# Three products by tokens: each tile takes all four units of weights in a row, then the other tile of its pair

## The chip, the cores and the metric

One Trainium2 chip, one of its NeuronCores. The metric is the device time of one execution in microseconds (us). The kernel before ran three times: 3430.88, 3432.21 and 3433.60 us, median 3432.21. One execution was taken by the hardware profiler; it ran 3431.43 us, and its profile covers a span of 3429.9 us.

## The reference, cut to what matters

The program computes two transformer-like blocks one after the other, on a sequence of 512 tokens with a model width of 1024. The first block has two layers of attention and MLP. The second block mixes three branches: a state-space branch (SSD), a delta-rule recurrence (RWKV) and a gated recurrence (HGRN). The change touches three slices of the second block's input product:

```
p = xn @ w_in[l]
z, xbc, dt_raw, p_rwkv, p_hgrn, p_gate = jnp.split(p, in_splits, axis=-1)
...
y = y.reshape(b, L, SSM_INNER) * jax.nn.silu(z)          # state-space branch
...
q, f_fwd, f_bwd, i, g = jnp.split(p, 5, axis=-1)          # gated recurrence; i are its values
```

`z` is 512 x 1024 and is made as two halves of 512 columns; the values `i` ("hgrn v") are 512 x 512. All are needed much later than they are made, so each is written to DRAM and fetched again when its branch ends.

## The kernel before

All matrix products take fp32 operands split in a high and a low part (both rounded to fp32r), and add three matmuls for each 128 rows of the inner dimension: high x high, high x low, low x high.

**Weights.** A class `Stream` brings the weights. They pass through six blocks of SBUF, in turn. Each block takes one load of 512 KB, called a unit here. SyncE issues the load (L381), ScalarE rounds the high part (L361, "split" in this text), VectorE subtracts to get the low part (L368). TensorE waits for the low part. A block is loaded anew only when the unit in it has been used for the last time: SyncE's queue waits on TensorE (mark `used`), and every later entry of that queue waits behind.

**Tokens and Features.** A product with tokens on the partitions is a `Tokens` job, one with features on them a `Features` job. The jobs touched have four units (256 rows of the inner dimension by 512 columns each) and four tiles of 128 tokens. A step is one unit for one tile: two chunks of 128 rows, three matmuls each (L427 to L429), so six matmuls of 512 columns. `together=2` means that the tiles go in two passes, tiles 0 and 1, then 2 and 3, and within a pass unit by unit, both tiles for each unit. A job has 16 steps. The banks of PSUM for these products are two, numbers 0 and 1 (ring "gemm 2"), handed out in turn: tile 2 takes the bank of tile 0, tile 3 that of tile 1, and the next job's first tile that of tile 2.

**Draining.** When a tile's last unit is done, `KeptOut` drains the bank into one of four staging tiles (`probabilities` twice, `gate0`, `gate1`) and SyncE stores it (L2180). For z, ScalarE takes tanh (L2199) and VectorE multiplies (L2208), which frees the bank. For hgrn v ScalarE copies (L2201) and that frees it.

**When units are split.** `Tokens.ahead` says up to which unit ScalarE and VectorE have split when the first tile of a pair takes a unit. In the last pass, at the last unit, it goes one unit further, to the third unit of the next job. That unit's load goes to the block of this job's first unit.

**What sets the order.** A `Plan` gives each step of each stage a time, in steps of products. Each engine's program is the list of all steps sorted by that time. TensorE's part of a scan stage may be put later by some steps (`later`). Beside the z products run pieces of the state-space scan (its decay matmuls L2568 and L2570, its L2601; on ScalarE L2620 and L2630; on VectorE L2668 and L2675), TensorE's share two steps later than the others'. Beside hgrn v run pieces of the RWKV scan, about one between any two steps (L2928, L2905, L2867 on TensorE, L3167 and L3188 on ScalarE, L3027 on VectorE), about one step later. Engines run their lists strictly in order, so a row that waits holds all rows behind it.

## Time and profile before

| what | value |
|---|---|
| median of three runs | 3432.21 us |
| profiled execution | 3431.43 us |
| its span | 3429.9 us |
| TensorE matmul busy | 3310.9 us (97%) |
| VectorE busy | 2018.7 us (59%) |
| ScalarE busy | 1354.2 us (39%) |
| load of a unit, issue to landing, median | 3.8 us |

The span is what the profiler saw, from the first to the last instruction. "Busy" is the time in which an engine had an instruction under way. Matmuls overlap: a matmul of 512 columns is shown with a length of 0.39 us, while one starts each 0.23 us when nothing stops them. The two z products run from 2280.78 us to 2354.5 us of the span, hgrn v from 2639.2 us to 2720.6 us.

### The profile page before, as it was taken

What the parts mean: (1) busy time and instruction counts of PE and PEld (TensorE: products, weight loads), DVE (VectorE), ACT (ScalarE), POOL (GpSimd) and SP (SyncE); (2) the same over time, 40 slices, a digit from 0 to 9 for tenths busy, and PEclk for the clock granted to TensorE, in tenths of its full rate; (3) what the DMA queues carried; (4) which work ended last, traced back from release to release, by engine and by line L of the source; (5) the groups of instructions that cost most, each with busy time, mean ns of one, the idle gap of its engine ahead of it and who ended that gap; (6) DMA issues with size and microseconds to landing.
All of it is one profiled execution on the core that took longest, in us unless ns stands there. A gap on an engine that the chain in (4) does not pass through costs nothing.

```text
span 3429.9 us, 53077 instructions
## 1 busy us (share of the span) xinstructions
PE 3310.9 (97%) x21864; PEld 2720.9 (79%) x21864; DVE 2018.7 (59%) x3803; ACT 1354.2 (39%) x2604; POOL 0.2 (0%) x4
## 2 busy tenths in 40 slices
PE   7989999999999999999999999999999999999998
PEld 7777788888888777788888888777777788888887
DVE  6776753554436776753554438775766678664434
ACT  5456543342225466543343224434443324232222
POOL 0000000000000000000000000000000000000000
PEclk9999999999999999999999999999999999999999
DMA  4221223233324221223233334333411235433332
GB/s 141 80 70 50 56 74 105 92 99 98 98 99 127 86 64 50 57 79 105 86 105 99 96 101 118 89 92 106 125 38 40 92 95 157 135 97 94 97 98 86
DMA packets 353875, 315.31 MB, mean 92 GB/s; under 512 B 10288, under 2 KB 281776, under 8 KB 353636
## 3 DMA queue, kind: packets, MB, share of 16 engines
q1 hardware_dynamic: 352916, 309.75, 29.9%
q8 instruction: 175, 2.87, 0.3%
q10 hardware_dynamic: 720, 2.16, 0.2%
q14 instruction: 64, 0.52, 0.0%
HBM read 288.28 MB, written 23.59 MB: 91 GB/s over the span
## 4 chain that ended last, share of the span: by engine, by line
PE 80%; DVE 11%; ACT 5%; issue 3%; DMA 2%; SPq 0%; DVEq 0%; ACTq 0%
PE banks L532 14%; PE banks L534 13%; PE banks L533 13%; PE banks L427 8%; PE banks L429 8%; PE banks L428 8%; DVE weights_r L368 2%; PE banks L632 1%; ACT weights_high_r L361 1%; PE banks L2928 1%; PE banks L2867 1%; PE banks L1241 1%; PE banks L1228 1%; PE banks L1332 1%; PE banks L2881 1%
## 5 line engine op out<-in xcount | busy, mean ns | idle before, releaser
L368 DVE TENSOR_TENSOR weights_r<-weights,weights_high_r 128x1024 fp32r<-128x1024 f32 (+2 forms) x517 | 592.9, 1154 | 355.7 <-ACT weights_high_r L361 354.6
L532 PE MATMUL banks<-h_T_hi,weights_high_r 128*128 128x512 f32 (+2 forms) x1912 | 759.6, 397 | 10.6 <-DVE h_T_lo L881 4.7
L534 PE MATMUL banks<-h_T_hi,weights_r 128*128 128x512 f32 (+2 forms) x1912 | 737.9, 386 | 0.0
L533 PE MATMUL banks<-h_T_lo,weights_high_r 128*128 128x512 f32 (+2 forms) x1912 | 737.5, 386 | 0.0
L361 ACT ACTIVATE weights_high_r<-weights 128x1024 fp32r<-128x1024 f32 (+2 forms) x517 | 511.2, 1000 | 360.8 <-DMA weights<-in_w_mlp 213.3
L532 PEld LDWEIGHTS banks<-h_T_hi,weights_high_r 128*128 128x128 f32 x1912 | 361.4, 189 | 98.6 <-issue 28.8
L534 PEld LDWEIGHTS banks<-h_T_hi,weights_r 128*128 128x128 f32 x1912 | 361.2, 189 | 72.7
L533 PEld LDWEIGHTS banks<-h_T_lo,weights_high_r 128*128 128x128 f32 x1912 | 361.7, 189 | 68.0 <-issue 2.6
L427 PE MATMUL banks<-weights_high_r,h_T_hi 128*128 128x512 f32 (+2 forms) x672 | 279.3, 416 | 9.2 <-DVE gate L2208 3.7
L429 PE MATMUL banks<-weights_high_r,h_T_lo 128*128 128x512 f32 (+2 forms) x672 | 254.9, 379 | 0.0
L428 PE MATMUL banks<-weights_r,h_T_hi 128*128 128x512 f32 (+2 forms) x672 | 254.7, 379 | 0.0
L602 DVE TENSOR_TENSOR cellsX<-cellsX,banks 128x512 f32<-128x512 f32 x112 | 76.7, 685 | 276.3 <-PE banks L429 276.2
L427 PE MATMUL banks<-weights_high_r,cellsM_r 128*128 128x512 f32 (+1 forms) x464 | 181.6, 391 | 0.0
L428 PE MATMUL banks<-weights_r,cellsM_r 128*128 128x512 f32 (+1 forms) x464 | 178.1, 384 | 0.0
L429 PE MATMUL banks<-weights_high_r,cellsC_r 128*128 128x512 f32 x432 | 169.2, 392 | 0.0
L427 PEld LDWEIGHTS banks<-weights_high_r,h_T_hi 128*128 128x128 f32 x672 | 127.6, 190 | 41.3 <-issue 9.7
L427 PE MATMUL banks<-weights_high_r,cellsE_r 128*128 128x512 f32 x384 | 150.3, 391 | 2.4 <-DVE cellsS L3898 2.4
L428 PE MATMUL banks<-weights_r,cellsE_r 128*128 128x512 f32 x384 | 150.0, 391 | 0.0
L429 PE MATMUL banks<-weights_high_r,cellsB_r 128*128 128x512 f32 x384 | 149.6, 390 | 0.0
L428 PEld LDWEIGHTS banks<-weights_r,h_T_hi 128*128 128x128 f32 x672 | 128.0, 190 | 23.2 <-issue 3.9
L429 PEld LDWEIGHTS banks<-weights_high_r,h_T_lo 128*128 128x128 f32 x672 | 127.5, 190 | 22.9
L1541 DVE TENSOR_TENSOR gate<-gate,banks 128x512 f32<-128x512 f32 x64 | 44.0, 687 | 131.2 <-ACT gate L1533 131.2
(562 smaller groups left out, 5228.5 us busy)
## 6 DMA issues: line engine op xcount, KB each, us to landing
weights<-in_w_in SPq DMA_DIRECT2D x183, 512.0 KB, 3.8
weights<-in_w_mlp SPq DMA_DIRECT2D x128, 512.0 KB, 3.8
weights<-in_ffn_w_in SPq DMA_DIRECT2D x44, 512.0 KB, 3.8
weights<-in_w_out SPq DMA_DIRECT2D x24, 512.0 KB, 3.6
weights<-in_ffn_w_down SPq DMA_DIRECT2D x22, 512.0 KB, 3.5
weights<-in_w_mem_kv SPq DMA_DIRECT2D x16, 512.0 KB, 3.5
weights<-in_w_diff_o SPq DMA_DIRECT2D x16, 512.0 KB, 3.6
weights<-in_w_mla_o SPq DMA_DIRECT2D x8, 512.0 KB, 3.4
```

Of the source, the lines that this page charges most:

```text
L361: ac.e.activation(self.part(c.w_high_r, u), self.part(c.w_raw, u), ACT.Copy).then_inc(*ac.tell("high", u))
L368: ve.e.tensor_tensor(self.part(c.w_raw_r, u), self.part(c.w_raw, u), self.part(c.w_high_r, u).bitcast(F32), ALU.subtract).then_inc(*ve.tel ...
L427: pe.e.matmul(out, lhsT=hi[k][:, tok], rhs=wh[:, j, :], start=(k == 0), stop=False)
L428: pe.e.matmul(out, lhsT=hi[k][:, tok], rhs=wl[:, j, :], start=False, stop=False)
L429: mm = pe.e.matmul(out, lhsT=lo[k][:, tok], rhs=wh[:, j, :], start=False, stop=last)
L532: pe.e.matmul(out, lhsT=wh[:, k, :], rhs=hi[k][:, cols], start=(k == 0), stop=False)
L533: pe.e.matmul(out, lhsT=wh[:, k, :], rhs=lo[k][:, cols], start=False, stop=False)
L534: mm = pe.e.matmul(out, lhsT=wl[:, k, :], rhs=hi[k][:, cols], start=False, stop=(k == self.chunks - 1))
L602: ve.e.tensor_tensor(dst, dst, got, ALU.add).then_inc(*ve.frees(*key))
L632: mm = pe.e.transpose(bank[0:m, at:at + rows], src, c.ident[0:rows, 0:rows])
L1228: mm = pe.e.matmul(bank[:, 0:v[j].shape[-1]], lhsT=c.pT[n % 2][:, j * P:(j + 1) * P], rhs=v[j], start=(j == 0), stop=(j == len(v) - 1))
L1541: ve.e.tensor_tensor(y, y, got, ALU.mult).then_inc(*ve.frees(*key))
```

## The change

`Tokens` gets a parameter `in_a_row`. The units are taken in groups of that many, and within a pass each tile takes a whole group before the other tile of the pair does. With 1, the default, the order is as before. The three jobs (`z 0`, `z 1`, `hgrn v`) are given 4, which is all their units. The other `Tokens` jobs keep 1.

```diff
-    def __init__(..., together=NT, tile_ready=lambda t: ()):
+    def __init__(..., together=NT, tile_ready=lambda t: (), in_a_row=1):
...
+        self.in_a_row = in_a_row
...
         for n, some in enumerate(self.passes):
-            for u in self.units:
+            for some_units in (self.units[j:j + self.in_a_row] for j in range(0, len(self.units), self.in_a_row)):
                 for t in some:
-                    yield n, u, t, t == some[0], u == self.units[-1]
+                    for u in some_units:
+                        yield n, u, t, t == some[0], u == self.units[-1]
...
-            return Tokens(c, name, c.hT, KD, w[:, col:col + 512], sink, ready=normed, ring=ring, together=2)
+            return Tokens(c, name, c.hT, KD, w[:, col:col + 512], sink, ready=normed, ring=ring, together=2, in_a_row=4)
```

Lines of the file behind it move down by one or two: L2199 is L2201 afterwards, L3167 is L3169. Steps of one job, before: u0t0 u0t1 u1t0 u1t1 u2t0 u2t1 u3t0 u3t1, then the same with t2 and t3. Now: u0t0 u1t0 u2t0 u3t0 u0t1 u1t1 u2t1 u3t1, then the same with t2 and t3. On TensorE and SyncE the rows read the same before and after, since a row names neither the unit nor the tile; their waits have other values. On ScalarE and VectorE rows move.

ScalarE, start of the second z product, before. L2199 drains tile 3 of the first z product. `weights4`, `weights5` and `weights0` are the blocks whose loads the splits wait for; L2630 and L2620 belong to the scan.
```order
L2199 ACTIVATE probabilities<-banks 128x512 [waits sp_kept1]
L361 ACTIVATE weights_high_r_50<-weights 128x1024 [waits sp_weights4]
L361 ACTIVATE weights_high_r_50<-weights 128x1024 [waits sp_weights5]
L2630 ACTIVATE cellsE<-banks 128x512 [waits pe_filled]
L2630 ACTIVATE cellsS<-banks 128x512 [waits pe_filled]
L2620 ACTIVATE cellsX_r_51<-small,cellsC 128x128 x4
L2620 ACTIVATE small_r_58<-small,cellsC 128x128 x4
L361 ACTIVATE weights_high_r_50<-weights 128x1024 [waits sp_weights0]
L2199 ACTIVATE gate0<-banks 128x512 [waits sp_kept2,pe_filled]
```
The same place now:
```order
L2201 ACTIVATE probabilities<-banks 128x512 [waits sp_kept1]
L361 ACTIVATE weights_high_r_50<-weights 128x1024 [waits sp_weights4]
L361 ACTIVATE weights_high_r_50<-weights 128x1024 [waits sp_weights5]
L361 ACTIVATE weights_high_r_50<-weights 128x1024 [waits sp_weights0]
L2632 ACTIVATE cellsE<-banks 128x512 [waits pe_filled]
L2632 ACTIVATE cellsS<-banks 128x512 [waits pe_filled]
L2622 ACTIVATE cellsX_r_51<-small,cellsC 128x128 x4
L2622 ACTIVATE small_r_58<-small,cellsC 128x128 x4
L2201 ACTIVATE gate0<-banks 128x512 [waits sp_kept2]
```
The split that waits for `weights0` moved up past the scan's four rows.

VectorE, the same place, before. L2208 frees the bank of tile 3, L368 are the low parts, L2675 and L2668 belong to the scan.
```order
L2208 SCALAR_TENSOR_TENSOR probabilities<-probabilities,banks 128x512 [waits act_tanh]
L368 TENSOR_TENSOR weights_r_49<-weights,weights_high_r_50 128x1024 [waits act_high] x2
L2675 TENSOR_TENSOR cellsE<-cellsE,cellsM 128x512 [waits bank4_freed]
L2668 TENSOR_TENSOR cellsE_r_56<-small,cellsC_r_55 128x512 [waits pe_filled]
L2675 TENSOR_TENSOR cellsS<-cellsS,cellsM 128x512 [waits bank5_freed]
L2668 TENSOR_TENSOR cellsS_r_57<-small,cellsC_r_55 128x512 [waits pe_filled]
L368 TENSOR_TENSOR weights_r_49<-weights,weights_high_r_50 128x1024 [waits act_high]
L2208 SCALAR_TENSOR_TENSOR gate0<-gate0,banks 128x512 [waits act_tanh]
```
Now:
```order
L2210 SCALAR_TENSOR_TENSOR probabilities<-probabilities,banks 128x512 [waits act_tanh]
L368 TENSOR_TENSOR weights_r_49<-weights,weights_high_r_50 128x1024 [waits act_high] x3
L2677 TENSOR_TENSOR cellsE<-cellsE,cellsM 128x512 [waits bank4_freed]
L2670 TENSOR_TENSOR cellsE_r_56<-small,cellsC_r_55 128x512 [waits pe_filled]
L2677 TENSOR_TENSOR cellsS<-cellsS,cellsM 128x512 [waits bank5_freed]
L2670 TENSOR_TENSOR cellsS_r_57<-small,cellsC_r_55 128x512 [waits pe_filled]
L2210 SCALAR_TENSOR_TENSOR gate0<-gate0,banks 128x512 [waits act_tanh]
```
The third low part moved up past the scan's four rows.

ScalarE, second pass of hgrn v, before. L3167 and L3188 belong to the RWKV scan, L2201 drains tile 2, `weights1` is the block of the job's first unit, loaded anew with the third unit of the next job.
```order
L3167 ACTIVATE cellsE<-banks 128x256 [waits pe_filled]
L3167 ACTIVATE cellsS<-banks 128x256 [waits pe_filled]
L3188 ACTIVATE cellsX<-banks 128x256 [waits pe_filled]
L3188 ACTIVATE probabilities<-banks 128x256 [waits pe_filled]
L3167 ACTIVATE cellsE<-banks 128x256 [waits pe_filled]
L3167 ACTIVATE cellsS<-banks 128x256 [waits pe_filled]
L3188 ACTIVATE cellsX<-banks 128x256 [waits pe_filled]
L3188 ACTIVATE probabilities<-banks 128x256 [waits pe_filled]
L3167 ACTIVATE cellsE<-banks 128x256 [waits pe_filled]
L3167 ACTIVATE cellsS<-banks 128x256 [waits pe_filled]
L2201 ACTIVATE probabilities<-banks 128x512 [waits sp_kept0]
L361 ACTIVATE weights_high_r_50<-weights 128x1024 [waits sp_weights1]
```
Now; the first two rows are the two that stand ahead of the first row above:
```order
L3169 ACTIVATE cellsE<-banks 128x256 [waits pe_filled]
L3169 ACTIVATE cellsS<-banks 128x256 [waits pe_filled]
L2203 ACTIVATE probabilities<-banks 128x512 [waits sp_kept0]
L361 ACTIVATE weights_high_r_50<-weights 128x1024 [waits sp_weights1]
L3169 ACTIVATE cellsE<-banks 128x256 [waits pe_filled]
L3169 ACTIVATE cellsS<-banks 128x256 [waits pe_filled]
L3190 ACTIVATE cellsX<-banks 128x256 [waits pe_filled]
L3190 ACTIVATE probabilities<-banks 128x256 [waits pe_filled]
L3169 ACTIVATE cellsE<-banks 128x256 [waits pe_filled]
L3169 ACTIVATE cellsS<-banks 128x256 [waits pe_filled]
```
The drain of tile 2 and the split behind it moved up past ten rows, three rounds of the scan.

VectorE, the same place, before. L3246 and L3027 belong to the scan.
```order
L3246 TENSOR_TENSOR cellsE<-cellsE,banks 128x256 [waits pe_filled]
L3246 TENSOR_TENSOR cellsS<-cellsS,banks 128x256 [waits pe_filled]
L3027 TENSOR_TENSOR cellsX<-banks,small 128x256 [waits pe_filled,act_taken]
L3027 TENSOR_TENSOR cellsX<-banks,small 128x256
L3027 TENSOR_TENSOR cellsX<-banks,small 128x256 [waits pe_filled,act_taken]
L3027 TENSOR_TENSOR probabilities<-banks,small 128x256
```
Now:
```order
L3248 TENSOR_TENSOR cellsE<-cellsE,banks 128x256 [waits pe_filled]
L3248 TENSOR_TENSOR cellsS<-cellsS,banks 128x256 [waits pe_filled]
L368 TENSOR_TENSOR weights_r_49<-weights,weights_high_r_50 128x1024 [waits act_high]
L3029 TENSOR_TENSOR cellsX<-banks,small 128x256 [waits pe_filled,act_taken]
L3029 TENSOR_TENSOR cellsX<-banks,small 128x256
L3029 TENSOR_TENSOR cellsX<-banks,small 128x256 [waits pe_filled,act_taken]
L3029 TENSOR_TENSOR probabilities<-banks,small 128x256
```
The low part of the same unit stands ahead of L3027 (now L3029). Before it stood behind three rounds of the scan as well.

## Rows read from the trace of the kernel before

**Rows 1.** The page: busy time of each engine, and the chain's shares.
```profile
PE 3310.9 (97%) x21864; PEld 2720.9 (79%) x21864; DVE 2018.7 (59%) x3803; ACT 1354.2 (39%) x2604; POOL 0.2 (0%) x4
...
PE 80%; DVE 11%; ACT 5%; issue 3%; DMA 2%; SPq 0%; DVEq 0%; ACTq 0%
```

**Rows 2.** TensorE in time: start us, length us, line, tiles, [idle before <-releaser].
```profile
2285.28 0.39 PE L427 MATMUL banks<-weights_high_r,h_T_hi 128*128 128x512 f32 x1
...
2296.00 0.50 PE L427 MATMUL banks<-weights_high_r,h_T_hi 128*128 128x512 f32 x1 [0.32 <-DVE gate L2208]
...
2300.08 0.50 PE L427 MATMUL banks<-weights_high_r,h_T_hi 128*128 128x512 f32 x1 [1.53 <-DVE gate L2208]
...
2311.09 0.47 PE L427 MATMUL banks<-weights_high_r,h_T_hi 128*128 128x512 f32 x1 [0.22 <-DVE probabilities L2208]
...
2318.94 0.50 PE L427 MATMUL banks<-weights_high_r,h_T_hi 128*128 128x512 f32 x1 [3.39 <-DVE probabilities L2208]
...
2326.62 0.55 PE L2601 MATMUL banks<-cellsE 128*128 128x64 f32 x4
...
2333.97 0.50 PE L427 MATMUL banks<-weights_high_r,h_T_hi 128*128 128x512 f32 x1 [0.82 <-DVE gate L2208]
...
2339.35 0.50 PE L427 MATMUL banks<-weights_high_r,h_T_hi 128*128 128x512 f32 x1 [1.06 <-DVE gate L2208]
...
2354.01 0.39 PE L429 MATMUL banks<-weights_high_r,h_T_lo 128*128 128x512 f32 x1
...
2354.54 0.47 PE L532 MATMUL banks<-h_T_hi,weights_high_r 128*128 128x512 f32 x1
```

**Rows 3.** VectorE in time, same columns, start of both z products.
```profile
2285.20 1.22 DVE L368 TENSOR_TENSOR weights_r<-weights,weights_high_r 128x1024 fp32r<-128x1024 f32 x1
...
2318.20 0.69 DVE L2208 SCALAR_TENSOR_TENSOR probabilities<-probabilities,banks 128x512 f32<-128x512 f32 x1 [3.35 <-ACT probabilities L2199]
2319.14 2.36 DVE L368 TENSOR_TENSOR weights_r<-weights,weights_high_r 128x1024 fp32r<-128x1024 f32 x2 [0.26 <-ACT weights_high_r L361]
2321.42 0.69 DVE L2675 TENSOR_TENSOR cellsE<-cellsE,cellsM 128x512 f32<-128x512 f32 x1
```

**Rows 4.** ScalarE in time, same columns, splits of weights in z.
```profile
2289.65 1.06 ACT L361 ACTIVATE weights_high_r<-weights 128x1024 fp32r<-128x1024 f32 x1 [11.00 <-DMA weights<-in_w_in]
...
2318.07 2.00 ACT L361 ACTIVATE weights_high_r<-weights 128x1024 fp32r<-128x1024 f32 x2
```

**Rows 5.** SyncE's queue in time, loads of weights in z.
```profile
2285.69 0.43 SPq L381 DMA_DIRECT2D weights<-in_w_in  x1
...
2319.30 0.43 SPq L381 DMA_DIRECT2D weights<-in_w_in  x1
```

**Rows 6.** TensorE in time, same columns, in hgrn v.
```profile
2687.40 0.40 PE L429 MATMUL banks<-weights_high_r,h_T_lo 128*128 128x512 f32 x1
...
2706.37 0.40 PE L429 MATMUL banks<-weights_high_r,h_T_lo 128*128 128x512 f32 x1
...
2708.51 0.41 PE L2928 MATMUL banks<-cellsE 64*64 64x64 f32 x16
2709.34 0.46 PE L2928 MATMUL banks<-cellsS 64*64 64x64 f32 x16 [0.41 <-DVE cellsX L3027]
```

**Rows 7.** Busy time by window: length, PE, PEld, DVE, ACT, POOL, PEclk, DMA.
```profile
2639.00:2724.00 85.00, 79.70 (x2219) 65.55 (x2215) 52.51 (x143) 27.56 (x72) 0.00 (x0) 1.00 0.13 37
```

**Rows 8.** SyncE's queue in time, in hgrn v.
```profile
2687.82 0.38 SPq L381 DMA_DIRECT2D weights<-in_w_in  x1
```

**Rows 9.** ScalarE in time, same columns, in hgrn v.
```profile
2707.22 0.39 ACT L3167 ACTIVATE cellsE<-banks 128x256 f32<-128x256 f32 x1 [5.04 <-PE banks L2928]
...
2718.81 1.07 ACT L361 ACTIVATE weights_high_r<-weights 128x1024 fp32r<-128x1024 f32 x1
```

**Rows 10.** VectorE in time, same columns, in hgrn v.
```profile
2708.53 0.76 DVE L3027 TENSOR_TENSOR cellsX<-banks,small 128x256 f32<-128x256 f32 x2 [2.10 <-ACT cellsX L3188]
```

**Rows 11.** Busy time by window, behind the longest wait in z.
```profile
2320.00:2324.00 4.00, 4.00 (x12) 3.17 (x11) 3.91 (x6) 0.06 (x1) 0.00 (x0) 0.57 0.65 175
```

More of the change, by code:

```diff
@@ L386, with __init__ @@
 class Tokens(Stage):
-    def __init__(self, c, tag, xT, chunks, src, sink, ready=(), tiles=NT, ring="gemm", together=NT, tile_ready=lambda t: ()):
+    def __init__(self, c, tag, xT, chunks, src, sink, ready=(), tiles=NT, ring="gemm", together=NT, tile_ready=lambda t: (), in_a_row=1):
         self.c, self.tag, self.xT, self.chunks, self.sink, self.ready, self.tiles = c, tag, xT, chunks, sink, ready, tiles
+        self.in_a_row = in_a_row
         self.ring, self.cols, self.tile_ready = ring, src.shape[1], tile_ready
```

## The prediction

> **What bounds the kernel now.** I read four views. First the page's busy times and the shares of the chain of waits: TensorE is busy 97% of the span and carries 80% of the chain [rows 1]. So an edit pays only where TensorE stands still, or where it makes TensorE stand still. Second, TensorE in order of time over the two z products. Six of their steps start late because the VectorE drain of a PSUM bank (L2208) was late: by 0.32, 1.53, 0.22, 3.39, 0.82 and 1.06 us, 7.34 us in all [rows 2]. The step after them, the first of the next gates, starts with no recorded idle, 0.30 us after the last matmul would have let it (2354.54 against 2354.01 plus 0.23). Third, the drains and weight splits on VectorE and ScalarE and the loads on SyncE around these steps [rows 3 to 5]. Fourth, the same for the product of the recurrence's values, "hgrn v". It has no wait for a bank; each of its steps lies between pieces of the RWKV scan, and TensorE is busy 79.70 of 85.00 us there at full clock, 2.4 GHz [rows 6, 7].
>
> **What the change does not do.** No matmul is added or removed, and the names and sizes of TensorE's and SyncE's instructions stay in place. A Tokens job has 16 steps of six matmuls, numbered 0 to 15 here: the pair (tile 0, tile 1), then the pair (2, 3), each over four units. What moves is when a bank is full, when a unit is first needed, when it is last used, and so where its drain and the splits of later units stand.
>
> **Bank waits removed.** Before, tile 0 is full after step 6 and its bank is wanted at step 8. Now it is full after step 3. Tile 1 is full after step 7 as before, but tile 3 wants its bank at step 12, not 9. A bank then has four steps to be drained instead of one. I remove all but the 0.22: tile 2 of the first z product is now full early, but ScalarE drains it behind the same scan work. Idle is counted from the modelled end of the last matmul; back to back, starts are 0.23 us apart and the modelled length is 0.39, so each wait that goes gives 0.16 more. First z: 0.32 + 1.53 + 2 x 0.16 = 2.2. Second z: its tile-1 start 3.39 + 0.16 = 3.6; then 0.82 + 1.06 + 2 x 0.16 = 2.2; and the 0.30 at its end. Removed in all: 8.3 us.
>
> **New wait 1, low part of the fourth unit, first z.** It was needed at step 6, now at step 3, which TensorE reaches at 2285.28 [rows 2]. VectorE makes it from 2285.20 for 1.22 us, to 2286.42 [rows 3]. Cost 1.2. VectorE is then itself fed by TensorE's next scan matmuls, so the delay is carried on and not made up. First z: 2.2 - 1.2 = 1.0 gained.
>
> **New waits 2 and 3, start of the second z.** Tile 1's late bank no longer stops step 1, but step 3 now wants the low part of unit 3. VectorE makes it right behind the late drain: from 2319.14, one of two halves of 2.36, so ready about 2320.4 [rows 3]. TensorE would have gone on at 2318.94 - 3.58 = 2315.4, and two steps of 1.37 take it to 2318.1: it waits 2.3 there. Then the splits of the units after next: in the order above the one that waits for weights0 has moved up on both engines, ahead of the scan's L2675. Its load is issued at 2319.30, behind the store of tile 3 [rows 5]. A load issued at 2285.69 let its waiting split start at 2289.65, 3.96 us later [rows 4, 5], so this one starts at 2323.26, takes 1.06, VectorE's half about 1.15, and L2675 starts at 2325.5 instead of 2321.42 and ends 0.69 later, at 2326.2. TensorE's L2601, which reads it, stood at 2326.62 [rows 2]. Of the 3.6 removed 0.4 is left. All this is relative to the scan matmuls before it, so the 1.0 of the first product stays on top. Sum of z: 1.0 + 0.4 + 2.2 + 0.3 = 3.9 us gained. Bounds: all 8.3 if neither queue was late; 0.5 if the price of a lowered clock (below) is added twice.
>
> **New wait 4, hgrn v.** This is the cost. Unit 0's block of weights is now used last in step 12 (tile 3), not step 9. The split of unit 6, whose load needs that block, moved the other way: from behind step 14 to behind step 11. On ScalarE it stood at 2718.81, behind three more rounds of the scan [rows 9]. Now it stands before the L3167 that ran at 2707.22 (L3169 in the changed file). Behind it in that queue are L3167 and L3188, on which TensorE's L2928 and VectorE's L3027 wait; VectorE's half stands before L3027 too. Step 12 ends at 2706.37 + 0.40 = 2706.77 [rows 6]. In the kernel before the load that waited for step 9 (last matmul 2687.40 + 0.40) was issued at 2687.82 [rows 6, 8]. So: issue 2706.8, landed and split begun 2710.75, VectorE's half 1.08 later (2318.07 to 2319.14 [rows 3, 4]) at 2711.8, L3027 at 2713.0 instead of 2708.53 [rows 10]: 4.4 late. TensorE's L2928 already waits 0.41 for L3027 [rows 6], so all of it reaches TensorE, and the steps behind it follow in one queue. Cost 4.4; at least 3.6, if only L2928's own wait for L3167 counts (2708.51 to about 2712.1), and at most 5.5, if one more VectorE half of 1.15 comes in front. That nothing of it shows is rival A.
>
> The Trainium skill ("DMA: Bandwidth & Descriptors", Rules for kernel authors) says to issue a DMA early, compute, and wait on its semaphore late; here both ends move the wrong way. That page's fit (Anatomy of one DMA) of 2.0 us plus bytes over 436 GB/s gives an estimate of 3.2 us for 512 KB where the trace has 3.96; by it wait 4 would be 3.7 and not 4.4. The measured duration is used.
>
> **Clock.** After the idle of 3.39 us the granted clock was 0.57 on average from 2320 to 2324 [rows 11], that is partly 1.2 GHz. The 24 matmuls from 2318.94 reached the next work at 2326.16 (0.46 before L2601's 2326.62), 7.2 us against 24 x 0.23 = 5.5 (two scan matmuls of 0.23 lie between): price 1.7. In hgrn v there is no lowered clock now [rows 7]. The new wait there is 3.6 us at one stroke (L2928 from 2708.51 to about 2712.1), longer than the 3.39. I take 1.7, between 0 and 1.7. At the start of the second z two waits of 2.3 and 2.6 replace one of 3.39; I take the lowering there as hidden under the wait for L2601 and count 0, between 0 and 1.7 lost.
>
> **Sum.** -3.9 + 4.4 + 1.7 = +2.2 us. Profiled execution: 3431.43 + 2.2 = 3433.6. It ran 0.8 below the median of the runs, 3432.21; on that basis 3434. A difference under 0.2% (6.9 us) can't be told from no change with this kernel.
>
> **Rivals.**
> A. *The banks win.* All 8.3 of the removed waits is gained and little comes back: the three new waits of z find cover, and ScalarE's order around hgrn v costs the 4.4. 3432.2 - 8.3 + 4.4 = 3428. With wait 4 covered too it is 3424, faster. For it: the idle rows are there. Against: the drain at 2318.20 and the split at 2319.14 are neighbours in one queue [rows 3], so removing one wait shows the other.
> B. *Slower by more than can be missed.* One mechanism: the early wait for unit 6 in hgrn v, with everything behind it in ScalarE's queue. It decides from 6.9 us net. If it costs its upper 5.5, the price of the clock comes twice in hgrn v (3.4) and z gives only 0.5, the time is 3432.2 + 8.4 = 3441. Against: one unit only is early; the next split stands behind step 15.
> C. *The reorder does nothing in z.* The scan's own chain between TensorE, ScalarE and VectorE sets the pace of the stage, and the bank waits are where its slack shows. Then the gain is 0 and hgrn v costs 4.4 to 6.1: 3437 to 3438. For it: L2601 waits on L2675 elsewhere in this stage. Against: VectorE stood idle 3.35 before the drain at 2318.20 [rows 3].
> D. *The clock gains.* The lowering at 2320 goes with the idle of 3.39 before it, the waits that replace it bring none, and the one in hgrn v brings none either. The lowered stretch at the start of the second z is hidden under the wait for L2601 in my sum, so here it counts only as a price that doesn't come in hgrn v and one that goes behind L2601: -3.9 + 4.4 - 1.7 = -1.2, 3431. Against: the new waits add up to more than the old one. The Trainium skill ("TensorE: Matmul & The Clock Gate", HAM oscillation) advises the same loop order, all units of one tile before the next wait, for the sake of the clock.
>
> **How the numbers follow.** Forecast 3434 (z between 0.5 and 5 gained, hgrn v between 3.6 and 6 lost): 0.50. D: 0.15, 3431. C: 0.15, 3437. A: 0.12, of it 0.04 faster than 3425.3. B: 0.08, 3441. The range 3428 to 3439 leaves out B and the fast third of A. Faster 0.04; slower 0.09, from B and the upper end of C; same 0.87.
>
> **What would show it.** In the changed profile: no L427 waiting for L2208 (then L2210) except once by about 0.2; a wait of about 1.2 at the fourth step of the first z product and about 2.3 at the fourth step of the second, put down to VectorE's L368; a wait of about 2.6 of L2601 behind it; in hgrn v a ScalarE L361 that waits 7 to 8 us for its DMA and, at the same moment, TensorE L2928 standing still 3 to 4 us. The prediction is wrong if that TensorE wait is under 2 us, if the fourth steps don't wait, or if the time between the start of z and the end of hgrn v changes by more than 7 us.

## The result, and the profile after: 0.2% slower, outside the range

The changed kernel took 3445.43 us, median of 15 runs (3433.22 to 3449.6), against 3433.85 for the kernel before, median of 15 runs on the same chip (3430.88 to 3443.37). The ratio is 1.002, 95% interval 1.0011 to 1.0029, that is 3.8 to 10.0 us slower. The two medians are 11.6 us apart; the ratio goes by all 15 runs of each, and this text goes by the ratio. The forecast was 3434, with a range of 3428 to 3439.

The profiled execution took 3442.14 us with a span of 3440.2. The page's busy times and shares of the chain:

```profile
PE 3320.1 (97%) x21864; PEld 2727.9 (79%) x21864; DVE 2019.9 (59%) x3803; ACT 1353.2 (39%) x2604; POOL 0.2 (0%) x4
...
PE 80%; DVE 10%; ACT 5%; issue 3%; DMA 2%; SPq 0%; DVEq 0%; ACTq 0%
```

The work is the same, 21864 matmuls, and the chain's shares are the same within a point [rows 1]. PE shows 9.2 us more busy time; matmuls at the lowered clock are longer: L2907's are shown at a median of 0.52 us where the clock is 1.2 GHz in hgrn v and 0.32 just ahead of it.

**z.** TensorE in time, every wait of over 0.5 us for a bank or for weights in the two z products, and the one that was to stay:

```profile
2292.78 0.50 PE L429 MATMUL banks<-weights_high_r,h_T_hi 128*128 128x512 f32 x1 [1.04 <-DVE weights_r L368]
...
2316.33 0.47 PE L429 MATMUL banks<-weights_high_r,h_T_hi 128*128 128x512 f32 x1 [0.22 <-DVE probabilities L2210]
...
2325.66 0.50 PE L429 MATMUL banks<-weights_high_r,h_T_hi 128*128 128x512 f32 x1 [2.05 <-DVE weights_r L368]
...
2331.85 1.10 PE L2603 MATMUL banks<-cellsE 128*128 128x64 f32 x8 [1.12 <-DVE cellsE L2677]
```

Of the bank waits [rows 2] only the one of 0.22 is left. The two at fourth steps are there and are put down to VectorE's low half, L368: 1.04 (forecast 1.2) and 2.05 (forecast 2.3). L2603, L2601 before, waits for L2677. SyncE's load ahead of that last wait:

```profile
2324.53 0.43 SPq L381 DMA_DIRECT2D weights<-in_w_in  x1
```

ScalarE's half of the split that wants it:

```profile
2328.88 1.06 ACT L361 ACTIVATE weights_high_r<-weights 128x1024 fp32r<-128x1024 f32 x1 [3.58 <-DMA weights<-in_w_in]
```

VectorE's half, and the scan's L2677 behind it:

```profile
2329.97 1.23 DVE L368 TENSOR_TENSOR weights_r<-weights,weights_high_r 128x1024 fp32r<-128x1024 f32 x1 [3.23 <-ACT weights_high_r L361]
2331.11 0.68 DVE L2677 TENSOR_TENSOR cellsE<-cellsE,cellsM 128x512 f32<-128x512 f32 x1
```

The load is issued at 2324.53, the split that wants it starts at 2328.88, 4.35 later, and the scan's L2677 stands behind it. In the kernel before, the scan's row came first [rows 3].

**hgrn v.** TensorE at the end of step 12 and behind it:

```profile
2709.26 0.39 PE L431 MATMUL banks<-weights_high_r,h_T_lo 128*128 128x512 f32 x1
...
2710.09 0.83 PE L2907 MATMUL banks<-cellsM,cellsE 64*64 64x192 f32 x16
2716.17 1.56 PE L2907 MATMUL banks<-cellsM 64*64 64x192 f32 x16 [5.25 <-ACT cellsE L3169]
```

SyncE, the load that waits for step 12:

```profile
2709.67 0.38 SPq L381 DMA_DIRECT2D weights<-in_w_in  x1
```

ScalarE, everything from 2704.93 to 2715.75:

```profile
2704.93 0.60 ACT L2203 ACTIVATE probabilities<-banks 128x512 f32<-128x512 f32 x1
2714.79 1.06 ACT L361 ACTIVATE weights_high_r<-weights 128x1024 fp32r<-128x1024 f32 x1 [9.25 <-DMA weights<-in_w_in]
2715.75 0.37 ACT L3169 ACTIVATE cellsE<-banks 128x256 f32<-128x256 f32 x1
```

VectorE:

```profile
2715.88 1.23 DVE L368 TENSOR_TENSOR weights_r<-weights,weights_high_r 128x1024 fp32r<-128x1024 f32 x1 [6.58 <-ACT weights_high_r L361]
2717.02 0.75 DVE L3029 TENSOR_TENSOR cellsX<-banks,small 128x256 f32<-128x256 f32 x2
```

Step 12 ends at 2709.65 and the load goes out at 2709.67; before, it went out behind step 9, at 2687.82 [rows 8]. ScalarE has stood still for 9.25 us for it. Behind its split comes L3169, which ran at 2707.22 before [rows 9]; TensorE waits 5.25 us for it. The wait falls on L2907, which fills the banks that L3169 empties and stands just ahead of the L2930 that I had named. Busy time by window behind that, with the columns of [rows 7]; the granted clock is the third number from the end:

```profile
2711.00:2714.00 3.00, 0.00 (x0) 0.00 (x0) 0.00 (x0) 0.00 (x0) 0.00 (x0) 1.00 0.62 172
2714.00:2717.00 3.00, 0.83 (x12) 0.68 (x16) 1.12 (x1) 1.88 (x4) 0.00 (x0) 0.73 0.01 1
2717.00:2720.00 3.00, 2.56 (x62) 2.21 (x56) 2.56 (x9) 0.38 (x1) 0.00 (x0) 0.50 0.00 0
2720.00:2723.00 3.00, 3.00 (x26) 2.34 (x22) 1.05 (x3) 0.00 (x0) 0.00 (x0) 0.63 0.00 0
```

TensorE is idle from 2711 to 2716.17; its clock falls late in that idle (0.73 on average from 2714 to 2717) and stays at 0.50, 1.2 GHz, while it works again. The kernel before had 1.00 through this whole stretch [rows 7].

**Where the time went.** In both traces I took the start of every matmul, counted from the first, and the change of the difference over each stretch (in us, against the profiled execution of before; "z, first" and "z, second" run from 2280.8 to 2312.5 and to 2354.4 in before's time, hgrn v's stretch from 2705.0 to 2723.9). "Whole" is the difference of the spans. "Low" is the whole time that the trace shows at 1.2 GHz.

```
kernel                    ahead of z  z,first  z,second  to 2440  hgrn v  whole   low
before                           0.0      0.0       0.0      0.0     0.0    0.0  53.5
after                            6.3     -1.1      -2.6     -0.1     7.6   10.3  75.0
after again                      9.0     -1.1       0.4      1.5     6.9   17.3  84.5
one in a row (control)           8.2      0.0       0.0      0.1     0.5   10.5  76.7
z alone                          6.9     -1.1       0.5      1.6     0.0    8.9  78.0
z alone, again                   1.1     -1.1       0.6      1.6     0.3    3.5  68.1
hgrn v alone                     5.2      0.0       0.7      0.0     9.0   18.1  86.5
all, old split steps             7.1     -1.1      -3.6      1.2     1.0    6.4  70.7
z, old split steps               7.2     -1.1      -5.2      1.2     0.0    2.1  64.1
z, old split steps, again        7.0     -1.1      -5.2      1.1     0.0    2.0  63.8
z, one split further             4.4     -1.1      -2.4      4.8     0.7    5.7  70.9
hgrn v, early splits only       -2.2      0.0      -0.1      1.3     0.3   -0.9  49.4
two in a row                     4.0     -1.5      -2.9     -0.1     0.0   -0.8  67.2
hgrn v, ScalarE early           -0.3      0.0       1.5      0.0     7.1    8.1  63.6
```

The column "ahead of z" compares work that the change does not touch. The control, with the order of before, differs there by 8.2 us, with 41.0 us at 1.2 GHz ahead of z against 23.9: that is scatter, and goes with the lowered clock, not with the edit. A whole span of one profile can't judge an edit of 5 us in this kernel; the stretches around the edit can better, and the many runs. The stretches scatter too: the second z product is unchanged in the control, in both kernels that change hgrn v's order alone and in the one with early splits only, and differs there by -0.1 to 1.5.

### The profile page after: what moved, and what is told of

It is laid out like the page before. It is cut to its first block, busy times and chain, and to the rows that moved or that the text cites. A ratio compares the mean times of both kernels' runs of the same rounds, so it can differ in the third digit from the quotient of the medians.

```text
span 3440.2 us, 53075 instructions
## 1 busy us (share of the span) xinstructions
PE 3320.1 (97%) x21864; PEld 2727.9 (79%) x21864; DVE 2019.9 (59%) x3803; ACT 1353.2 (39%) x2604; POOL 0.2 (0%) x4
## 4 chain that ended last, share of the span: by engine, by line
PE 80%; DVE 10%; ACT 5%; issue 3%; DMA 2%; SPq 0%; DVEq 0%; ACTq 0%
PE banks L534 14%; PE banks L536 13%; PE banks L535 13%; PE banks L429 9%; PE banks L431 8%; PE banks L430 8%; DVE weights_r L368 2%; PE banks L634 1%; ACT weights_high_r L361 1%; PE banks L2869 1%; PE banks L2930 1%; PE banks L1230 1%; PE banks L1243 1%; PE banks L1334 1%; PE banks L2883 1%
## 5 line engine op out<-in xcount | busy, mean ns | idle before, releaser
L368 DVE TENSOR_TENSOR weights_r<-weights,weights_high_r 128x1024 fp32r<-128x1024 f32 (+2 forms) x517 | 593.2, 1155 | 358.8 <-ACT weights_high_r L361 357.7
L534 PE MATMUL banks<-h_T_hi,weights_high_r 128*128 128x512 f32 (+2 forms) x1912 | 762.1, 399 | 10.0 <-DVE h_T_lo L883 4.2
L534 PEld LDWEIGHTS banks<-h_T_hi,weights_high_r 128*128 128x128 f32 x1912 | 364.0, 190 | 98.2 <-issue 28.5
L604 DVE TENSOR_TENSOR cellsX<-cellsX,banks 128x512 f32<-128x512 f32 x112 | 76.7, 685 | 273.5 <-PE banks L431 273.4
L430 PEld LDWEIGHTS banks<-weights_r,h_T_hi 128*128 128x128 f32 x672 | 127.7, 190 | 23.2 <-issue 3.9
```

The costliest lines, as they stand in the source:

```text
L368: ve.e.tensor_tensor(self.part(c.w_raw_r, u), self.part(c.w_raw, u), self.part(c.w_high_r, u).bitcast(F32), ALU.subtract).then_inc(*ve.tel ...
L430: pe.e.matmul(out, lhsT=hi[k][:, tok], rhs=wl[:, j, :], start=False, stop=False)
L534: pe.e.matmul(out, lhsT=wh[:, k, :], rhs=hi[k][:, cols], start=(k == 0), stop=False)
L604: ve.e.tensor_tensor(dst, dst, got, ALU.add).then_inc(*ve.frees(*key))
```

## The experiments

Each kernel ran 8 to 12 times beside the kernel before on the same chip, and one execution of each was profiled. The ratios compare runs of one chip; the median of the kernel before was 3437.40, 3435.50, 3434.33 or 3437.43 us, by chip, so the times below are not compared with each other.

**Which job costs: z alone, hgrn v alone, and a control.** The edit, with the control's value behind it:

```diff
-..., together=2, in_a_row=4)
+..., together=2, in_a_row=4 if tag == "z" else 1)   # z alone
+..., together=2, in_a_row=1 if tag == "z" else 4)   # hgrn v alone
+..., together=2, in_a_row=1)                        # control
```

Z alone, first run, was expected to do this:

> Units in a row for the two z products alone, hgrn v as before. Theory 1 (the split of the next job's third unit, moved ahead of its load in hgrn v, is what costs; z gains): between the start of z and 2600 us TensorE's matmuls come 3.5 to 4 us earlier than in the kernel before, nothing changes in hgrn v, time 3.7 us under the kernel before. Rival 2 (the long rows of matmuls, or something ahead of z that the changed program brings, cost several us everywhere): slower than the kernel before, with 4 us or more lost ahead of z, as in the changed kernel's profile (+6.3 us ahead of 2250 us). Rival 3 (z's gain is given back later): the matmuls are back at the old distance by 2600 us.

Hgrn v alone:

> Units in a row for hgrn v alone. Theory 1: nothing changes in z; in hgrn v one stall of TensorE of 5 us and the lowered clock behind it, 7.5 us together, time 7.5 us over the kernel before. Rival 2: the loss is spread, several us are lost ahead of z. Rival 4 (in hgrn v the long wait of ScalarE is harmless and the loss came with the shift from z): under 2 us lost in hgrn v.

The control:

> The changed file with in_a_row=1 for all three: the same instructions as the kernel before, lines moved by two. Theory 1: same time as the kernel before within the scatter (1 to 2 us between medians), and the profile differs from it only by where the clock is lowered; single runs scatter by 10 us. Rival 2 in its form 'something that comes with the file': 3 us or more slower.

Measured: z alone 3436.24 us, ratio 1.0001 (0.9992 to 1.0011); hgrn v alone 3445.19, ratio 1.0024 (1.0014 to 1.0034); the control 3435.45, ratio 0.9997 (0.9987 to 1.0006). The loss is all in hgrn v. TensorE's longest wait there, with hgrn v alone (total, times, longest):

```profile
PE banks L2907 <- ACT cellsE L3169: 5.6, 1, 5.6
```

It is the changed kernel's wait again, and the sum of the two ratios' differences, 0.0001 + 0.0024, is about that of both together (0.0020). But z alone didn't bring its gain of some 4 us. In its profile, TensorE at L2603 of the second z:

```profile
2331.84 1.97 PE L2603 MATMUL banks<-cellsE 128*128 128x64 f32 x8 [2.63 <-DVE cellsE L2677]
```

Busy time and granted clock by window there:

```profile
2324.00:2330.00 6.00, 3.50 (x14) 2.55 (x14) 2.58 (x4) 2.48 (x4) 0.00 (x0) 1.00 0.50 131
2330.00:2336.00 6.00, 4.16 (x18) 3.97 (x18) 3.59 (x5) 1.60 (x5) 0.00 (x0) 0.64 0.00 0
2336.00:2342.00 6.00, 6.00 (x23) 4.92 (x23) 3.09 (x5) 2.21 (x7) 0.00 (x0) 0.80 0.12 44
```

The clock is full up to 2330, so TensorE reaches L2603 early and waits 2.63 us, and then it works at a lowered clock, 0.64 and 0.80 on average, for parts of 12 us. In the profile of the changed kernel the lowered part lay ahead of L2603, behind the wait of 2.05, and hid over half of that wait (1.12 left):

```profile
2326.00:2330.00 4.00, 4.00 (x12) 3.13 (x11) 0.77 (x2) 1.06 (x1) 0.00 (x0) 0.57 0.47 128
```

Why the clock fell early in one execution and late in the others is open.

**The product order without the move of the splits.** TensorE's order and the drains stay as in the changed kernel; the splits of loaded weights, on both engines, go back to the steps they had:

```diff
-        for n, u, t, first, final in self.steps():
-            if first and not final:
+        for (_, _, t, _, final), (n, u, _, first, last) in zip(self.steps(), self.steps(1)):
+            if first and not last:
                 self.c.stream.act(self.ahead(n, u))
```

Here steps takes the number in a row as its argument, so that the second list is the old one. In all three jobs:

> TensorE's order and the drains as in the changed kernel, for all three products, but ScalarE and VectorE split weights at the steps at which the kernel before splits them. Theory 1: the ScalarE wait for a load in hgrn v goes and with it the 7.5 us; in z the wait of about 1 us for the fourth unit stays in the first product, the one of 2 us in the second stays, the one for L2603 goes (1.1 us and a lowered clock): z gains 4 to 6 us, time 4 to 6 us under the kernel before. Rival 5 (it is the later last use of unit 0 that costs, whatever the place of the split): hgrn v still loses 5 us or more. Rival 2: slower than before.

In z only, with hgrn v as before:

> z in the changed order of products, its splits of loaded weights at the steps they had before, hgrn v as before. Theory 1: the gain of z alone, -4 to -5 us in the two stretches of z, 0 in hgrn v; 3 to 5 us faster than before by the runs (ratio 0.9985 to 0.999). Rival 3 (what z gains is given back later, by lowered clock or at the scan): the stretches of z 4 us shorter and the whole unchanged (ratio within 0.0005 of 1).

Measured: 3434.47 us, ratio 0.9988 (0.9977 to 0.9999) for all jobs; 3432.94, ratio 0.9987 (0.9978 to 0.9995) for z only. The stall in hgrn v is gone (1.0 us, 0.5 in the control), though the last use is as late as in the changed kernel. In z, the trace of the second kernel. ScalarE's split that waited 3.58 us, now behind the scan's rows:

```profile
2334.39 1.05 ACT L361 ACTIVATE weights_high_r<-weights 128x1024 fp32r<-128x1024 f32 x1
```

TensorE's waits for L2677 from 2240 to 2440 (us in all, times, longest):

```profile
PE banks L2603 <- DVE cellsE L2677: 5.0, 5, 1.6
```

The same three windows as for z alone:

```profile
2324.00:2330.00 6.00, 3.95 (x20) 3.22 (x20) 5.42 (x7) 2.10 (x3) 0.00 (x0) 1.00 0.47 131
2330.00:2336.00 6.00, 6.00 (x34) 5.17 (x34) 1.22 (x2) 4.67 (x12) 0.00 (x0) 1.00 0.00 0
2336.00:2342.00 6.00, 5.94 (x35) 4.87 (x34) 4.37 (x8) 1.68 (x3) 0.00 (x0) 1.00 0.13 46
```

The split finds its weights landed, L2603 waits no longer than 1.6 at a time anywhere there, and the clock stays at 1.00. In the kernel with all three jobs at the old steps L2603 doesn't wait at this place either, but its clock was lowered, behind the wait of 2.06 for the fourth unit:

```profile
2324.00:2330.00 6.00, 4.13 (x11) 3.31 (x12) 5.10 (x7) 1.50 (x2) 0.00 (x0) 0.72 0.48 131
```

It gains 4.7 in z where the other gains 6.3. The changed kernel's first profile, with its clock lowered at the same place, gained 3.7: the 1.0 between them is about its wait of 1.12 at L2603. So in z too the early split took back part of what the banks gave: always the wait at L2603, and in three of four profiles the lowered clock behind it. The old steps don't keep the clock full by themselves.

**Was that chance?** Both z kernels once more, unedited, on one chip:

> The z part alone with its splits following the new order, again, beside the run with the splits at their old steps on the same chip. Open is why z's gain did not show in this kernel's runs (ratio 1.0001) and did with the old splits (0.9987). If the place of the splits decides: ratio 0.9995 to 1.001 again, with a lowered stretch of 6.83 us behind the 2.05 us wait and z1 no shorter than before. If it was chance (where lowered stretches fall in a run): ratio 0.9980 to 0.9995, like its neighbour.

> The z part with the splits at their old steps, again. If the place of the splits decides: ratio 0.998 to 0.9992, and at least 0.0006 below its neighbour. If it was chance: the two agree within 0.0005. In both cases z0 1.1 us shorter and z1 3 to 5 us shorter than before in the profile unless a lowered stretch falls into it.

Measured: 3435.22 us, ratio 0.9996 (0.9984 to 1.0009), with the splits that follow the new order; 3432.19, ratio 0.9987 (0.9978 to 0.9996), with the old steps. Their profiles repeat the first ones to 0.1 us in both z stretches, with a wait at L2603 of 2.7 us and lowered clock behind it in the one and neither in the other. By the profiles the place of the splits decides. The runs lean the same way, by 0.0009 and 0.0014, but in each pair the intervals overlap. Taken together, the 23 runs with the splits that follow average 0.9998 of the kernel before on their chips, and the 22 with the old steps 0.9987, an estimate of mine from the means with a 95% interval of 0.0004 to 0.0018 for the difference.

**Is the early split enough, or the late last use?** Products in the order of before in all three jobs; in hgrn v alone the splits stand at the changed kernel's steps (self.steps(4) in the loop above):

> The order of products before in all three jobs; only in hgrn v the splits of loaded weights stand at the changed kernel's steps, three steps earlier for the third unit, while the buffers come free as early as before. Theory 1 (the stall needs both: the late last use, which holds the load, and the early split, which puts ScalarE and VectorE behind it): 0 to 2 us in hgrn v. Rival 5 (the early place of the split is enough): 4 to 8 us there and a ratio of 1.001 to 1.0025. Rival 6 (the late last use is enough) was told apart by the run with the splits as before (+1.0 us there).

Measured: 3434.87 us, ratio 1.0001 (0.9992 to 1.001), 0.3 us in hgrn v. SyncE's load, the first of two issues in its row:

```profile
2686.21 14.10 SPq L381 DMA_DIRECT2D weights<-in_w_in  x2
```

ScalarE's split of it:

```profile
2700.90 1.06 ACT L361 ACTIVATE weights_high_r<-weights 128x1024 fp32r<-128x1024 f32 x1
```

The load has 14.7 us before its split comes up, and the split waits for nothing. With the kernel above, which had the late use and not the early split, this shows that neither alone costs; the two together do.

**Through which queue.** Hgrn v in the changed order, ScalarE's half of the splits early, VectorE's half where it was before:

> hgrn v alone in the changed order of products; of the splits of loaded weights only ScalarE's halves stand early as in the changed kernel, VectorE's stand where they were before; z as before. Theory 1 in its narrow form (the stall reaches TensorE through ScalarE's queue: split waits for the load, the emptying of a bank behind it waits for the split): the stretch of hgrn v is as long as with both early, +6 to +9 us, ratio 1.0015 to 1.003. Rival 7 (VectorE's queue hands it on): 0 to 2 us.

Measured: 3442.77 us, ratio 1.0019 (1.0008 to 1.003), 7.1 us in hgrn v. TensorE's longest wait:

```profile
PE banks L2907 <- ACT cellsE L3169: 5.5, 1, 5.5
```

ScalarE's half:

```profile
2711.67 1.06 ACT L361 ACTIVATE weights_high_r<-weights 128x1024 fp32r<-128x1024 f32 x1 [9.50 <-DMA weights<-in_w_in]
```

VectorE, the scan's row and its half:

```profile
2713.58 0.76 DVE L3029 TENSOR_TENSOR cellsX<-banks,small 128x256 f32<-128x256 f32 x2 [7.66 <-ACT cellsX L3190]
...
2725.96 1.22 DVE L368 TENSOR_TENSOR weights_r<-weights,weights_high_r 128x1024 fp32r<-128x1024 f32 x1
```

VectorE's half comes 14 us behind ScalarE's, at 2725.96, and the stall is as long as with both early. ScalarE's queue alone hands it to TensorE; VectorE only waits with it. The mirror image, VectorE's half early and ScalarE's late, has no run: VectorE would wait for a ScalarE half that stands behind work which waits for VectorE.

**The changed kernel again**, to part scatter from effect:

> The changed kernel once more, unedited. Theory 1 (the split of the next job's third unit, moved ahead of its load, stops TensorE in hgrn v): about +7.6 us in the stretch of hgrn v again and -3.7 us in the two stretches of z, 5 to 10 us slower than before in all (ratio 1.0015 to 1.003). Rival 2 (what ran ahead of z is slower by the change): the +6.3 us seen ahead of z comes again; by theory 1 that part is scatter and changes size or sign.

Measured: 3444.7 us, ratio 1.0017 (1.0005 to 1.0029). The loss in hgrn v comes back (6.9), the gain in z does not: it is the picture of z alone, with 2.48 us at L2603 and the lowered clock behind. Ahead of z it was 9.0 slow, against 6.3 in the first profile and 8.2 in the control: no effect of the edit. So the first profile, in which z gained 3.7, was the exception among the four profiles of this form of z.

**Further and less.** First, z with its old split steps and the last splits one unit further, to take the 2.05 us wait at the second z's fourth step away:

```diff
-            far = last + (3 if u < last else 1 + AHEAD)
+            far = last + (3 if u < last else 1 + AHEAD + self.more)   # more=1 in z
```

> As the z part with its old splits, and the last-pass splits of z reach one unit further, so that the split for the second unit of the following job comes before the rows of the scan on VectorE. Theory 1: the 2 us wait at the start of the second z goes as well, -6 to -7 us in the stretches of z, ratio about 0.998. Rival: the third unit's split stands in front of a row of the scan that TensorE waits for then, and the wait only changes its name: -4 us, as without it.

Measured: 3433.29 us, ratio 0.9989 (0.998 to 0.9999), no better than without it. TensorE's waits in 2240 to 2440, second and third of the list:

```profile
PE banks L534 <- DVE probabilities L2210: 1.8, 1, 1.8
PE banks L429 <- DVE weights_r L368: 1.0, 1, 1.0
```

The 2.05 is gone, but the first of the list, L2603 for L2677, has grown from 5.0 to 6.4. At the start of the second z, one more split stands ahead of L2677 on VectorE, and TensorE waits there where it didn't without it:

```profile
2317.94 1.12 PE L2603 MATMUL banks<-cellsE 128*128 128x64 f32 x8 [1.87 <-DVE cellsE L2677]
```

Behind it the clock is lowered, 0.57 from 2318 to 2324. That is the rival's outcome, the wait changed its name. The wait of 1.8 is a further one, at the first drain (L2210) that the next job, the gates, needs (L534): the stretch up to 2440 is 4.8 longer, against 1.2. Second, two units in a row instead of four (in_a_row=2) in all jobs, the splits following:

> Two units in a row instead of four in all three jobs, with the splits of loaded weights following the order as in the changed kernel. Then the buffer of the first two units of hgrn v is free one step earlier than with four in a row, and the third unit's split stands two steps later relative to the load. Theory 1: the stall in hgrn v is small, 0 to 3 us against +6.9 to +9.0, and z keeps a gain of 2 to 5 us; ratio 0.9985 to 1.0005. Rival 2 (any row of units on one tile costs in hgrn v): 4 us or more there, ratio above 1.001.

Measured: 3431.77 us, ratio 0.9987 (0.9977 to 0.9997), 0.0 us in hgrn v and 4.4 gained in z. ScalarE's split in hgrn v:

```profile
2713.42 1.06 ACT L361 ACTIVATE weights_high_r<-weights 128x1024 fp32r<-128x1024 f32 x1
```

Busy time and granted clock in one window around it:

```profile
2700.00:2722.00 22.00, 20.53 (x586) 16.85 (x578) 10.83 (x28) 6.36 (x17) 0.00 (x0) 1.00 0.24 63
```

Its load went out at 2693.67, 19.8 us earlier, so the split waits for nothing, and the clock stays full. Unit 0's block is last used in step 10 here, two steps earlier than with four in a row and not one, as the expectation has it.

## Why the prediction was wrong

The order of events was right nearly everywhere; the sum was not, by two of its terms, both costs taken too small. The forecast difference was +2.2 us; the runs have 6.9, between 3.8 and 10.0. The term at fault by most is the lowered clock at the start of the second z, put at 0; the other is wait 4 in hgrn v, 4.4 for 5.6. Of my own signs of being wrong, the wait in hgrn v is there, but with 5.25 and not 3 to 4 us, and from the start of z to the end of hgrn v the profiles differ from before by 4.1 and, repeated, by 7.3, just over the 7 that I had allowed.

**Bank waits removed.** Right: five of six gone, the 0.22 left.

**New waits 1 and 2.** Right: 1.04 and 2.05 for 1.2 and 2.3. The first z gained 1.1, forecast 1.0, in every profile with four in a row.

**New wait 3.** The 2.6 forecast at L2603 is what three of four profiles show (2.63, 2.48, 2.7). The wrong step is the one on the clock beside it: "I take the lowering there as hidden under the wait for L2601 and count 0". That holds only in the first profile of the changed kernel, so its second z, 2.6 gained for 2.9, came out right by luck. In the other three the lowered clock follows this wait and falls on work. There the second z is 0.4 to 0.6 slower where I had 2.9 gained (0.4 + 2.2 + 0.3), a miss of 3.3 to 3.5, twice the 1.7 that I took as the most it could lose.

**New wait 4.** Right in place and in cause: late last use and early split in one, shown by taking away either. Step 12's last matmul stands at 2709.26, 2.89 later than before [rows 6], so on before's time the load was issued at 2709.67 - 2.89 = 2706.8, as forecast. The size was off: the forecast took 3.96 us from issue to the waiting split, from a load in z; here it was 5.12, so 1.2 more. The estimate of 3.2 us beside it was further off still: the fit of the Trainium skill ("DMA: Bandwidth & Descriptors", Anatomy of one DMA) that it is worked out from is stated for transfers that GpSimd issues, and SyncE issues these. L3029 came at 2717.02 - 2.89 = 2714.1 instead of 2708.53 [rows 10], 5.6 late: the 4.4 and the 1.2, just over my upper bound of 5.5.

**Clock in hgrn v.** The stretch lost 7.6, so beside the 5.6 there is 2.0, forecast 1.7. With hgrn v alone it was 9.0 in all. Forecast for the stretch 6.1; the four profiles with the stall have 6.9 to 9.0.

**The sum.** With hgrn v at 6.9 to 7.6 and z at -3.7 (once) or -0.7, forecast -3.9, the balance of the two profiles is 7.6 - 3.7 = +3.9 and 6.9 - 0.7 = +6.2, and not +2.2. The runs say +3.8 to +10.0, and +1.7 to +10.0 when repeated. Another 1.5 us lies behind the second z in the profiles with the late lowered stretch, against 1.1 to 1.3 in four others without it, so I ascribe none of it to the change.

**The rivals.** B, "slower by more than can be missed", had the mechanism and nearly the sum: a higher price of wait 4, the clock charged more than once, and z giving 0.5. I gave it 0.08, because I asked each of these to be at its bound by chance. They were not independent: in all four profiles with the stall in hgrn v the lowered clock came with it. A, C and D fell: z's banks did not win, the reorder did do something in z (with old split steps some 4.5 us of it stay), and the clock did not gain. C's number for z, nothing gained, is near what three of four profiles show (0.5 to 0.7), but not for C's reason: bank waits went, and other waits and a lowered clock took their place. The loop order that D names from the Trainium skill ("TensorE: Matmul & The Clock Gate", HAM oscillation) is advised there for products of few rows. In these profiles it brought the lowered clock into hgrn v, where there was none before. The Trainium skill ("DMA: Bandwidth & Descriptors", Rules for kernel authors), which the prediction cited on issuing early and waiting late, agrees with the runs: of the two moves, keeping either one as it was is enough.

**What the place of the splits is worth.** Four in a row with old split steps, or two in a row, is 0.13% faster than before (0.9987; 0.9978 to 0.9995 and 0.9977 to 0.9997), about 4.5 us. That is what is left of the 8.3 us of bank waits when the waits for the fourth units are paid. The prediction held that under 0.2% can't be told from no change with this kernel; these intervals exclude 1.

## What to carry to other kernels

When an order of products is changed, write down for each weight buffer the step of its last use and, separately, the place in each in-order queue of the first instruction that waits for its next load; moving them towards each other by even a few steps puts everything behind that instruction on the load's latency. Let the two follow different orders if need be: the products in the new order, the splits at their old steps. When a new wait of TensorE is priced, add the lowered clock behind it as part of the same event, not as a separate chance, and widen the range for it: at the two places looked at here it came with each of the waits between 2.48 and 5.65 us, and with some of those of about 2.

## What the runs showed of the hardware that I had not expected

**The same load, two latencies.** The 512 KB load in hgrn v, issued behind step 9 and behind step 12; each row is the median from issue to landing, for its one load. Before:

```profile
weights<-in_w_in SPq DMA_DIRECT2D x1, 512.0 KB, 3.7
```

After:

```profile
weights<-in_w_in SPq DMA_DIRECT2D x1, 512.0 KB, 5.1
```

It took 3.7 to 4.0 us in all eight profiles in which it was issued behind step 9 (before, the control, hgrn v with early splits only, and the five that change z alone), 5.1 to 5.5 in the five profiles with it behind step 12, the split late or early, and 4.4 with two in a row. Its shape is the same. The traces narrow the cause down. In the changed kernel, in the first 3 us behind the issue (2709.67 to 2712.67), a second queue has one packet of 16 KB:

```profile
q8 instruction: 1, 0.02, 1.9%
```

In the profile of before no such packet stands in the same stretch (2687.82 to 2690.82). It is there in all six profiles in which the load took 4.4 or more, and in none of the eight with 3.7 to 4.0. A load ends with sixteen landings. In the changed kernel fifteen of them came 3.39 to 3.92 us after the issue and one at 5.09; before, all sixteen came between 3.36 and 3.72. So one part of the load is late, and the fetch of instructions beside it is the likely reason. That the two went through the same DMA engine isn't in the trace, and no run moved the fetch, so it isn't shown.

**The clock.** The control, whose instructions stand as in before:

```profile
core 0: 3440.5 us, clock 0.989
```

Its clock is 0.989 against 0.992 in the profile of before, its TensorE was at 1.2 GHz for 76.7 us against 53.5, and at half speed 23.2 us more cost up to 11.6 (an estimate): that fits the 10.5 by which it is longer. Yet over many runs the two kernels are alike (0.9997). So single executions of this kernel differ by some 10 us by how long the clock is lowered, twice what the new order of z is worth.
